# A 2.6 MB transfer changes queue: the bias table's skewed copies go out from Pool instead of from the queue that loads the weights

## The reference

```
x += 1/2 * gate1 * SwiGLU_1(mod1(rms(x)))
h = mod2(rms(x));  aq, ak, av, iq, ik, iw, gq, gk, gv, gz, gb, ga = split(h @ w_in)
x += gate2 * W_out [ SparseAttn(...) | GatedDeltaNet(...) ]
x += 1/2 * gate3 * SwiGLU_2(mod3(rms(x)));  y = rms(x) * norm_final

sparse attention, per block of 128 queries:
  score  = sum_h iw_h * relu(iq_h . ik / 8);  idx = top_k(score)
  logits = q . k[idx] / 8 + rel_bias[rel_bucket(idx - qpos)];  p = softmax(logits);  out = p @ v[idx]
```

## Time and profile before

| | |
|---|---|
| median of 3 runs | 1709.98 us (1709.63 to 1712.41) |
| the profiled execution | 1712.22 us, its span 1710.5 us |
| PE busy | 1531.2 us, 90% of the span |
| DVE busy | 694.0 us, 41% |
| ACT busy | 501.9 us, 29% |
| Pool busy | 130.6 us, 8% |
| q1 (SP's queue) | 192128 packets, 102.48 MB, 21.7% of 16 DMA engines |
| q0 (Pool's queue) | 12816 packets, 46.85 MB, 7.8% |
| mean granted PE clock | 0.949 |

### The profile page before, as it was taken

One profiled execution on the slowest core, in us unless ns is written; L12 is line 12 of the kernel. 1 busy time (PEld: TensorE's weight loads), 2 busy tenths in 40 slices (PEclk: granted clock), 3 DMA queues, 4 the chain that ended last, 5 costly groups with the idle time before them and its releaser, 6 DMA issues. The chain is left out here.

```text
span 1710.5 us, 29328 instructions
## 1 busy us (share of the span) xinstructions
PE 1531.2 (90%) x11814; PEld 1427.3 (83%) x11818; DVE 694.0 (41%) x1261; ACT 501.9 (29%) x850; POOL 130.6 (8%) x163
## 2 busy tenths in 40 slices
PE   5899999999999646998997988759799999999996
PEld 3899999999999646987895766549699999999996
DVE  3522332223224601788576655434522332233233
ACT  3533112211223402433323333422533112211234
POOL 2200000000002400000002220102200000000000
PEclk9999999999999777999998999879899999999998
DMA  8534335344214154222103021122122222222221
GB/s 311 163 123 159 124 114 169 111 131 152 74 58 143 33 65 89 82 50 52 48 2 118 21 60 32 44 77 78 44 80 74 74 74 74 74 70 74 72 63 67
DMA packets 205042, 150.70 MB, mean 88 GB/s; under 512 B 17620, under 2 KB 189941, under 8 KB 204945
## 3 DMA queue, kind: packets, MB, share of 16 engines
q1 hardware_dynamic: 192128, 102.48, 21.7%
q0 software_dynamic: 12816, 46.85, 7.8%
HBM read 140.06 MB, written 9.24 MB: 87 GB/s over the span
## 5 line engine op out<-in xcount | busy, mean ns | idle before, releaser
L2473 PE MATMUL pair<-h_hi,w_hi 128*128 128x320 f32 x1888 | 438.1, 313 | 41.0 <-ACTq L797 37.5
L2473 PE MATMUL pair<-h_hi,w_lo 128*128 128x320 f32 x1888 | 433.2, 311 | 0.0
L2473 PE MATMUL pair<-h_lo,w_hi 128*128 128x320 f32 x1888 | 433.2, 311 | 0.0
L280 DVE TENSOR_TENSOR w_lo<-w_raw,w_hi 128x1024 fp32r<-128x1024 f32 x174 | 213.2, 1226 | 383.0 <-ACT w_hi L275 371.2
L2473 PEld LDWEIGHTS pair<-h_hi,w_hi 128*128 128x128 f32 x1888 | 317.6, 190 | 55.3 <-issue 51.3
L2473 PEld LDWEIGHTS pair<-h_lo,w_hi 128*128 128x128 f32 x1888 | 318.6, 189 | 0.0
L2473 PEld LDWEIGHTS pair<-h_hi,w_lo 128*128 128x128 f32 x1888 | 318.2, 189 | 0.0
L275 ACT ACTIVATE w_hi<-w_raw 128x1024 fp32r<-128x1024 f32 x174 | 182.8, 1053 | 364.8 <-PE pair L2473 176.7
L407 DVE SCALAR_TENSOR_TENSOR x_t<-pair,gate,x_t 128x320 f32 (+1 forms) x112 | 49.0, 479 | 218.7 <-PE pair L2473 154.7
L2473 PE MATMUL pair<-a_hi,w_hi 128*128 128x320 f32 x528 | 121.8, 312 | 2.2 <-DVEq L417 2.2
L2473 PE MATMUL pair<-a_hi,w_lo 128*128 128x320 f32 x528 | 120.3, 309 | 0.0
(11 more groups left out here) (370 smaller groups left out, 1661.8 us busy)
## 6 DMA issues: line engine op xcount, KB each, us to landing
w_mod_raw<-w_mod POOLq DMA_DIRECT2D x28, 1024.0 KB, 7.8
w_raw<-ffn_w_gate SPq DMA_DIRECT2D x44, 512.0 KB, 3.8
w_raw<-ffn_w_up SPq DMA_DIRECT2D x44, 512.0 KB, 3.8
w_raw<-ffn_w_down SPq DMA_DIRECT2D x32, 512.0 KB, 4.1
w_raw<-w_in SPq DMA_DIRECT2D x24, 512.0 KB, 3.7
w_raw<-ffn_w_down SPq DMA_DIRECT2D x16, 384.0 KB, 3.5
w_mod_a<-w_mod POOLq DMA_DIRECT2D x4, 1024.0 KB, 10.7
w_mod_b<-w_mod POOLq DMA_DIRECT2D x4, 1024.0 KB, 24.0
```

What stands on the lines that cost most here:

```text
L280: dve.tensor_tensor(w_lo[:, u % HL], w_raw[:, u % RAW], w_hi[:, u % HL].bitcast(F32), ALU.subtract).then_inc(lo_done, 1)
L2473: mm = pe.matmul(pair[u % 2][0:width, b, 0:HALF], w[:, 0:width], x_parts[part][:, k, b * HALF:(b + 1) * HALF], start=(k == 0 and v == 0), ...
```

## The change

The transfer and its wait for the table leave `mix_loads`, where they stood ahead of the load of unit 6, and go to `mix_pool`, behind the eight loads of the index-key cache and ahead of the wait for the `tm` units. The access patterns, the source, the destination and the semaphore stay.

```diff
@@ -632,10 +632,6 @@
                 else:
                     parts = [(0, P, {"iq": W_IQ, "tm": W_AV, "g": W_GQ, "gz": W_GZ, "ak": W_AK}[kind] + i * P)]
-                if v == 6:
-                    sp.wait_ge(S["tbl"], 2)
-                    sp.dma_start(bass.AP(skewed.tensor, skewed.offset, [[P * (REL + 1), AH], [REL + 1, P], [1, REL]]),
-                                 tbl[0:AH].unsqueeze(1).broadcast_to([AH, P, REL])).then_inc(S["tbl_out"], 16)
                 for n_, (at, wd, col) in enumerate(parts):
                     s = raw_in[u % RAW] if n_ == len(parts) - 1 else S["raw_extra"]
                     sp.dma_start(dst[:, :, at:at + wd], w[:, :, col:col + wd]).then_inc(s, 16)
@@ -685,6 +681,9 @@
             for b in range(NB):
                 pool.dma_start(ik_raw[:, b], a["cache_idx_k"][0, b].rearrange("(k p) d -> p k d", p=P)).then_inc(S["ik_in"], 16)
+            pool.wait_ge(S["tbl"], 2)
+            pool.dma_start(bass.AP(skewed.tensor, skewed.offset, [[P * (REL + 1), AH], [REL + 1, P], [1, REL]]),
+                           tbl[0:AH].unsqueeze(1).broadcast_to([AH, P, REL])).then_inc(S["tbl_out"], 16)
             pool.wait_ge(S["tm"], 3)
```

## The result

The changed kernel takes 1715.39 us, the median of 12 runs (1712.67 to 1717.74), against 1710.52 us for the kernel before in 12 runs beside them. The ratio is 1.0028 with a 95% interval of 1.0019 to 1.0037: slower by 4.9 us. That is under 0.3%, but the interval does not reach 1. The forecast was 1713.9 us, 3.9 us over before, in a range of 1705.5 to 1720.

What follows compares the result with a forecast made beforehand. PE was taken as the bound except in its hole, waiting on late weights. Copies ending at 650.95 put unit 5's end at 670.07 instead of 666.17: 1709.98 + 3.9 = 1713.9 us, range 1705.5 to 1720.

Steps and rivals of the forecast that it cites:

- hole: PE's long wait for ACT to release a PSUM pair: 37.5 us before, forecast one unit earlier and 41.4 us.
- unit 4 cold, unit 5 warm: PE after the hole: unit 4 at a lowered clock in 9.76 us, then unit 5 at full pace in 7.05 us.
- Rival 1: Copies begin late or in smaller packets, unit 5's weights land first, unit 6's become the bound: -2 us, 1708; chance 0.19.
- Its other arm: Rival 1 with copies going one row a packet (0.416 us), unit 5's weights landing before about 643: -1.3 to -4.0 us.
- Rival 2: Weights not held up by the copies on the shared engines, PE's hole goes: -40 us, 1670; chance 0.10.
- Rival 3: Copies run slower from Pool's queue, 69 us if 1.3 times longer: +20 us, 1730; chance 0.11.
- the first: Rule: a source of 8 partitions sits on two ports, about 54 GB/s, whoever issues it and however many engines take part.
- The second: Rule: 9 to 17 descriptors a packet, so unit 5's load is only a sixth through when the copies end: +5.5 us.
- upper bound of +5.8 us: The sum if weight packets add to the copies' duration, making it 55.1 us instead of 53.2.

Runs made afterwards that it cites:

- sp_ahead_of_5: The kernel before, with the copies still on SP's queue but issued ahead of the load of unit 5 instead of unit 6: ratio 1.0025 to before, 1715.1 us.
- pool_after_5: The changed kernel, with Pool issuing the copies only once unit 5's weights have landed: ratio 0.9972 to the kernel before, 1707.7 us.
- act_queue: The changed kernel, with the copies issued by ACT on its own queue ahead of its split of unit 5: ratio 0.9984 to the kernel before, 1708.9 us.
- spread16_pool: The changed kernel, with the table on 16 partitions (each head twice) as source of the copies: ratio 0.9879 to the kernel before, 1691.4 us.
- spread128_pool: The changed kernel, with the table on all 128 partitions (each head 16 times), copies from Pool's queue: ratio 0.9765 to the kernel before, 1671.3 us.

## Why the prediction was right

| step | forecast | measured |
|---|---|---|
| Pool issues the copies after the table is complete | 0.31 us | 0.30 us (594.73 to 595.03) |
| issue of the copies to their first packet | 1.6 us | 1.8 us (595.03 to 596.84) |
| lead over unit 5's first packet | 0.25 us | 0.54 us |
| first to last packet of the copies | 53.2 us | 53.15 us (596.84 to 649.99) |
| from there to ACT's split of unit 5 | 0.4 us, an estimate | 0.6 us (649.99 to 650.56) |
| packets, copies to weights | 1 to 1, two rows each | 348 to 348, 5.1 KB |
| Pool's issue to ACT's split of unit 5, in all | 55.2 us | 55.5 us (595.03 to 650.56) |
| from the split to PE's return | 1.91 us | 1.91 us (650.56 to 652.47) |
| hole | 41.4 us, from the end of unit 3 | 41.6 us, from the end of unit 3 |
| unit 4 cold, unit 5 warm | 9.76 + 7.05 us | 9.52 + 7.04 us (652.47, 661.99, 669.03) |
| table complete to evacuation of unit 5 | +3.9 us | +4.0 us |
| total | +3.9 us | +4.9 us (+3.2 to +6.3 by the interval) |

The mechanism came out as forecast, step by step. That the sum meets the trace within 0.1 us is in part luck: the way to the split was 0.3 us longer than forecast and the two units were 0.25 us shorter.

The step that carried the sign was the order: Pool is free when the table is ready, so the copies begin just ahead of unit 5's weights, where they had begun just behind them. sp_ahead_of_5 shows this order alone to cost the same, and pool_after_5 shows that undoing it on Pool's queue turns the loss into a gain. The second step was what two queues on one engine do to each other, which the counts of the earlier trace rows gave, and the same counts hold, within 5%, in four kernels here (348 to 348, 300 to 287, 462 to 462, 854 to 845). It says what the queues do once the turns have begun; that they can begin 12 to 14 us late, as in act_queue and spread16_pool, the prediction did not have. In the changed kernel they ran from 606 us at the latest (19 packets to 19 until 608).

Rival 1 (unit 5 slips through) did not happen by itself; made to happen, it went further than I had priced it, since unit 6 went through as well. Its other arm, one row a packet, is act_queue: -2.7 us, where -1.3 to -4.0 was worked out, though unit 5's weights came 15 us later than that arm has them. Rival 2 had the right prize with the wrong way to it: the 40 us were to be had, but by more source partitions, not by another queue. Rival 3 is out: the copies ran at 1.78 MB / 36 us = 49.4 GB/s from Pool's queue, and at 49.3 from SP's.

Of the two rules that the prediction weighed, the first fits all runs: the issuer and the number of engines left the rate of 8 partitions at 49 to 53 GB/s, and more partitions raised it. The second would have left most of unit 5's load behind the copies, and that did not come: a packet of the copies held two rows. Its +5.5 us also took the large packets to be the copies' alone; with as many rows in the weights' packets, unit 5 would have been through about halfway, which is the case of rival 1. One slip: the forecast's own range ends at 1716.5, but its upper bound of +5.8 us gives 1709.98 + 5.8 = 1715.8; nothing else hangs on it.

The total is 1 us above the sum. The interval covers that, and no run here tells whether anything but scatter is in it.

## What to carry to other kernels

Moving a long transfer to another queue does not take it out of the way of the loads: on a shared engine, a load of n packets waited in these runs for about n packets of the long one, however small its own were. First count how long the transfer lasts and why; here a source on 8 partitions made 2.6 MB last 53 us, and spreading it over 128 partitions, with one small copy and table matmuls that took 0.2 us more a pair, was worth 41 us, eight to ten times the best gain from its place (pool_after_5: 4.8 us by the ratio, 4.1 by the medians). If the long transfer must stay, what counts is which load is the first to be caught: let through, by a wait if need be, those whose consumers are next.

## What the runs showed that I had not expected

- Two transfers of Pool's queue issued 1.1 us apart ran at the same time, on 8 engines each (96.6% of 16 engines busy), and the time of each packet rose from 0.81 to 1.48 us.
- With the copies on ACT's queue, SP's weight packets on the shared engines stood for some 14 us before the one-for-one turns began (23 packets of q1 from 605 to 611 us). In spread16_pool, with all 16 engines shared, the first weight packet moved at 609.5, 12 us after the copies' first. Why is open.
- Pool's queue counts 1040 packets more in the changed kernel (13856 against 12816), where 512 packets of two rows were moved there. In the page's line on packets those under 512 B rose by 519 (17620 to 18139). In the trace these are 512 packets of 8 bytes, moved from 596.9 to 599.0; pool_after_5 has as many, spread16_pool and spread128_pool have none. They have no cost that shows.
- The granted clock during the matmuls of the table differed between two executions (1.00 and 0.50; 0.70 against 1.23 us for a pair), which shifts everything behind by a microsecond and hides as much of a change of 4 us in a single profile.
